# A gated-MLP stage in which four more pieces of the up projection move high and low input side by side, and every such piece runs its high weights before its low ones

## What is computed

```
def conv_gated_mlp(h, w_up, conv_w, w_down):
    u = h @ w_up                                   # 256 x 1024 times 1024 x 5632
    up = jnp.pad(u, ((0, 0), (pad, pad), (0, 0)))
    u = sum(up[:, t:t + S] * conv_w[t] for t in range(CONV_WIDTH))   # width 3
    gate, val = jnp.split(u, 2, axis=-1)
    return (jax.nn.gelu(gate, approximate=True) * val) @ w_down
...
for l in range(DEPTH):
    ...
    h = rms_norm(x, ffn_pre_norm[l])
    x = x + rms_norm(conv_gated_mlp(h, ...), ffn_post_norm[l])
```

## Time and profile before

| | us |
|---|---|
| median of 3 runs | 1020.44 |
| lowest, highest | 1019.81, 1020.45 |
| the profiled execution's own time | 1019.93 |
| its span, first to last instruction | 1018.1 |

### The profile page before, as it was taken

One profiled execution on the slowest core, in us unless ns is written; L12 is line 12 of the kernel. 1 busy time (PEld: TensorE's weight loads), 2 busy tenths in 40 slices (PEclk: granted clock), 3 DMA queues, 4 the chain that ended last, 5 costly groups with the idle time before them and its releaser, 6 DMA issues.

```text
span 1018.1 us, 14973 instructions
## 1 busy us (share of the span) xinstructions
PE 1004.8 (99%) x5744; PEld 880.4 (86%) x5744; DVE 711.1 (70%) x963; ACT 582.5 (57%) x863; POOL 128.8 (13%) x245
## 2 busy tenths in 40 slices
PE   8999999999999999999999999999999999999997
PEld 7889999888888988888888899998888889888886
DVE  6535566555586898989875355666545869898986
ACT  6657666555446655555575666565653456555552
POOL 3343124000001000000025231230000020000000
PEclk9999999999999999999999999999999999999999
DMA  7554345544445665555454544464335545655541
GB/s 243 198 174 157 124 129 180 168 166 158 136 141 166 205 230 176 196 195 178 150 178 158 173 127 125 140 222 154 131 130 186 183 147 188 214 200 191 182 165 42
DMA packets 108907, 170.74 MB, mean 168 GB/s; under 512 B 3249, under 2 KB 72676, under 8 KB 108836
## 3 DMA queue, kind: packets, MB, share of 16 engines
q1 hardware_dynamic: 107676, 166.88, 50.3%
q10 hardware_dynamic: 1080, 2.63, 0.7%
q0 software_dynamic: 80, 0.26, 0.1%
HBM read 168.72 MB, written 1.05 MB: 167 GB/s over the span
## 4 chain that ended last, share of the span: by engine, by line
PE 97%; DVE 1%; DMA 1%; ACT 0%; DVEq 0%; SPq 0%; issue 0%; POOL 0%; POOLq 0%
PE bank L1473 21%; PE bank L1475 20%; PE bank L1474 20%; PE high_banks L1483 10%; PE high_banks L1481 5%; PE high_banks L1913 2%; PE high_banks L1473 2%; PE high_banks L1474 2%; PE high_banks L1475 2%; PE high_banks L1480 1%; PE high_banks L1814 1%; PE high_banks L1835 1%; PE high_banks L1906 1%; PE high_banks L1823 1%; PE high_banks L1851 1%; PE high_banks L1858 1%
## 5 line engine op out<-in xcount | busy, mean ns | idle before, releaser
L1095 DVE TENSOR_TENSOR w_lo<-w_raw,w_hi 128x2048 fp32r<-128x2048 f32 (+3 forms) x174 | 365.1, 2100 | 162.8 <-ACT w_hi L721 162.7
L721 ACT ACTIVATE w_hi<-w_raw 128x2048 fp32r<-128x2048 f32 (+3 forms) x174 | 305.0, 1754 | 152.1 <-PE high_banks L1483 96.5
L1473 PE MATMUL bank<-w_hi,hT 128*128 128x512 f32 (+3 forms) x716 | 263.3, 368 | 2.0 <-DVE hT L1123 1.1
L1475 PE MATMUL bank<-w_hi,hT 128*128 128x512 f32 (+3 forms) x716 | 257.5, 360 | 0.0
L1474 PE MATMUL bank<-w_lo,hT 128*128 128x512 f32 (+3 forms) x716 | 257.1, 359 | 0.0
L1473 PEld LDWEIGHTS bank<-w_hi,hT 128*128 128x128 f32 x716 | 134.6, 188 | 18.4 <-issue 3.0
L1483 PE MATMUL high_banks<-hT,w_hi 128*128 128x512 f32 x420 | 149.7, 396 | 0.0
L1475 PEld LDWEIGHTS bank<-w_hi,hT 128*128 128x128 f32 x716 | 134.5, 188 | 14.0
L1474 PEld LDWEIGHTS bank<-w_lo,hT 128*128 128x128 f32 x716 | 134.7, 188 | 12.9
L1481 PE MATMUL high_banks<-hT,w_lo 128*128 128x256 f32 x480 | 124.0, 279 | 0.0
L1481 PEld LDWEIGHTS high_banks<-hT,w_lo 128*128 128x128 f32 x480 | 90.5, 188 | 5.2
(11 more groups left out here) (252 smaller groups left out, 1477.2 us busy)
## 6 DMA issues: line engine op xcount, KB each, us to landing
w_raw<-in_w_up_dram SPq DMA_DIRECT2D x44, 1024.0 KB, 5.0
w_raw<-in_w_in_dram SPq DMA_DIRECT2D x36, 1024.0 KB, 5.0
w_raw<-in_w_in_dram SPq DMA_DIRECT2D x36, 768.0 KB, 4.3
w_raw<-in_w_down_dram SPq DMA_DIRECT2D x22, 1024.0 KB, 4.8
w_raw<-in_w_out_dram SPq DMA_DIRECT2D x8, 1024.0 KB, 4.9
w_raw<-in_w_in_dram SPq DMA_DIRECT2D x8, 672.0 KB, 4.1
w_raw<-in_w_branch_mla_dram SPq DMA_DIRECT2D x4, 1024.0 KB, 4.9
w_raw<-in_w_branch_diff_dram SPq DMA_DIRECT2D x4, 1024.0 KB, 5.0
```

The source lines that it names most:

```text
L721: nc.scalar.activation(w_hi[:, n % RING, 0:nk * cols], raw[:, n % RING, 0:nk * cols], ACT.Copy).then_inc(hi_done, 1)
L1095: V.tensor_tensor(w_lo[:, n % RING, s], raw[:, n % RING, s], w_hi[:, n % RING, s].bitcast(F32), ALU.subtract).then_inc(lo_done, 1)
L1473: PE.matmul(dst, lhs[1], rhs_hi, start=start, stop=False)
L1475: return PE.matmul(dst, lhs[0], rhs_hi, start=False, stop=stop)
```

## The change

BESIDE goes from 6 to 2: up 2 to up 5 become wide, on TensorE and on VectorE. All wide pieces (up 2 to up 20) go through a new function, `up_beside`, which in each half issues the eight matmuls of the high weights and then the eight of the low ones. A wide piece waits for `hi_done` (ScalarE's part) at its start, and for `lo_done` (VectorE's part) only ahead of its first low matmul. The counts of `up_summed` follow BESIDE.

```diff
-BESIDE = 6
+BESIDE = 2
...
-            def passes_beside(dst, w_parts, k):
-
-                if k == 0:
-                    PE.matmul(dst, w_parts[0], hT[:, k, :, :], start=True, stop=False)
-                last = PE.matmul(dst[:, 0:SEQ], w_parts[1], hT_hi[:, k, :], start=False, stop=False)
-                if k:
-                    last = PE.matmul(dst, w_parts[0], hT[:, k, :, :], start=False, stop=k == KD - 1)
-                return last
+            def up_beside(l, n, c):
+
+                hi, lo = cut(w_hi, n), cut(w_lo, n)
+                for j in range(2):
+                    dst, cols = up_banks(c)[:, j, :], slice(j * P, (j + 1) * P)
+                    for k in range(KD):
+                        PE.matmul(dst, hi[:, k, cols], hT[:, k, :, :], start=k == 0, stop=False)
+                    if j == 0:
+                        pe.wait_ge(lo_done, l * NPIECE + (n + 1 + RING))
+                    for k in range(KD):
+                        last = PE.matmul(dst[:, 0:SEQ], lo[:, k, cols], hT_hi[:, k, :], start=False, stop=k == KD - 1)
+                last.then_inc(piece_used, 1)
...
-                pe.wait_ge(lo_done, l * NPIECE + (n + 1 + RING))
+                if kind == "up" and beside(c):
+                    pe.wait_ge(hi_done, l * NPIECE + (n + 1))
+                else:
+                    pe.wait_ge(lo_done, l * NPIECE + (n + 1 + RING))
```

More of the change, by code:

```diff
@@ L1623, in use_piece @@
                         pe.wait_ge(up_summed, l * (LAST_UP - BESIDE) + (c - 1 - BESIDE))
+                    if beside(c):
+                        up_beside(l, n, c)
+                        return
                     for k, j in [(k, j) for j in range(2) for k in range(8)]:
                         w_parts = (hi[:, k, j * P:(j + 1) * P], lo[:, k, j * P:(j + 1) * P])
[L1626 to L1629, removed]
+                        last = passes(up_half(c, j), w_parts, hT_hi[:, k, :], hT_lo[:, k, :], k == 0, k == 7)
                     last.then_inc(piece_used, 1)
```

## The result

| | before | after |
|---|---|---|
| median | 1020.26 | 1026.47 |
| lowest, highest (6 runs each) | 1019.63, 1020.55 | 1025.77, 1026.88 |
| the profiled execution | 1019.93 | 1026.45 |

The ratio is 1.0059, with a 95% interval of 1.0049 to 1.0069: the change costs 6.2 us. The forecast was 1025.2, the range 1022.4 to 1028.0.

What follows compares the result with a forecast made beforehand. TensorE was taken to bound the kernel, with VectorE nearly full from up 2 to up 5. Per layer +2.9 us at down 1 less 0.5 for the order, +2.4; both layers +4.8, giving 1025.2 us; range 1022.4 to 1028.0.

Steps and rivals of the forecast that it cites:

- The bound and the mechanism: TensorE, busy 99%, bounds the kernel; from up 2 nearly full VectorE gets more work and delays down 0 and down 1.
- TensorE's saving: Up 2 to up 5 wide: 0.68 us per layer in the old order; 1.44 with the new order on all wide pieces.
- Rivals 1 and 2: Down 0 and down 1 not held up, 1017.5 to 1019.0, chance 0.09; or smaller waits, a draw, 1018.5 to 1022.4, 0.09.
- The walk along VectorE's row: Up 2 to down 1: extra sums delay `g_lo`, so TensorE waits 2.5 us at down 0, 1.3 at down 1; 2.9 late.
- VectorE without a gap from up 2 to up 7: A sign expected in the new profile: VectorE's row runs on from up 2 to up 7, its earlier waits used up.
- The order of high and low: In wide up pieces, high then low makes a piece 5.55 us, not 5.59: 0.04 each, 0.5 us per layer after down 1.
- the second of the signs of being wrong: Wide up pieces stay at 5.59 us: the order brings nothing, and the time is 1 us above the forecast.
- Rival 4: More waits at up 6 or up 7, or the order gains nothing or costs: +5.8 to +7.5, 1026.2 to 1028; chance 0.16.
- The waits in both layers, and none later: TensorE waits about 2.5 us ahead of down 0 and 1.3 ahead of down 1, in both layers, and none later.
- rival 3: The wait at down 0 brings the 1.2 GHz clock: up to 5.5 us a time, 1030 or 1036; chance 0.04.

Runs made afterwards that it cites:

- experiments 5 and 6: The changed kernel, then the kernel before, each without VectorE's four convolution operations on up 2 to up 5: 1018.89 us and 1020.48 us.
- experiment 3: The kernel before, with an extra unused VectorE sum of about 1.3 us after the scaling of each of up 2 to up 5: 1026.55 us, ratio 1.0061.
- experiment 1: The changed kernel with BESIDE back at 6, so only the order of high and low in the 15 old wide pieces differs from before: 1020.11 us.
- experiment 9: The changed kernel with g_lo of pairs 0 and 1 and down 0's split moved earlier in VectorE's row: 1026.41 us, ratio 1.0063.
- experiment 8: The changed kernel with `gated` and `g_lo` of the first nine pairs moved from VectorE to GpSimd: 1022.89 us, ratio 1.0029.
- experiment 2: The kernel before with BESIDE 2: up 2 to up 5 wide, in the old order and with the old wait: 1026.50 us, ratio 1.0060.
- experiment 4: The kernel before with a smaller extra VectorE operation, some 0.6 us, on each of up 2 to up 5: 1020.59 us, ratio 1.0002.
- experiment 7: The changed kernel with BESIDE 4: up 2 and up 3 narrow, in other PSUM banks: 1021.50 us, ratio 1.0010.
- experiment 10: The changed kernel with BESIDE 5: only up 5 wide in addition, up 2 to up 4 narrow: 1020.12 us, ratio 0.9996.

## Why the prediction was right

**The bound and the mechanism.** Right. TensorE's saving is real (experiments 5 and 6) and worth nothing, since VectorE's row decides when down 0 and down 1 start (experiment 3). Rivals 1 and 2 are out.

**The walk along VectorE's row.** With the 0.48 us taken off, `g_lo` of pair 0 starts at 361.9 (forecast 362.10), down 0 at 362.7 (362.9), `g_lo` of pair 1 at 379.93 (379.9), down 1 at 380.8 (380.7). The sum and the product last 1.92 us on up 4 (358.24 to 360.16), and so on all four pieces; for up 2 and up 4 I had 2.01, from a row in which VectorE had just waited. That is 0.2 us less by `g_lo`. The 0.45 us gap with the name "issue" ahead of up 5's convolution was used up, as taken; one like it that I had not foreseen, 0.43 us, opened in up 4's (364.44), in the first layer only, so that the two errors nearly cancel at down 1. That this start came out to 0.1 us is luck in part. By the starts, TensorE was ready for down 0 four times 5.58 us after up 2, at 360.87, and waited 2.27 us (the profile's 2.09 counts from a modelled end); forecast 2.5. Ahead of down 1 it was 1.23 for 1.3.

**VectorE without a gap from up 2 to up 7.** Right but for that 0.43 us; it waits for TensorE first at up 8 (0.66 us, at 392.52).

**The order of high and low.** This step failed, and it is the second of the signs of being wrong that the prediction names (1 us above the forecast; it was 1.3). I gave it 0.04 us a piece, from the duration of a matmul in a down piece, and so 0.5 us back in each layer after down 1. The pieces last 5.58 us, 0.01 less than before, and experiment 1 gives nothing. The layer is late by 3.0 us at down 2 as at down 1, and by 497.76 - 494.34 - 0.48 = 2.9 us where down 8 starts, right behind the last up piece: next to nothing comes back. With this term at 0.1 instead of 0.5 the sum is 2 x 2.8 = 5.6 us. The mis-sized price is that of a 512 in an up piece: eight take 340.39 - 338.55 = 1.84 us, 0.230 each, not the 0.227 of a down piece, which moves other operands. With the eight 256s in 0.95 us that is 0.349 us a pair, against the 0.35 of before; 0.003 us on 16 matmuls was all that I had built the gain on.

**The size.** Forecast +4.8, measured +6.2. Of the 1.4 between them 0.8 are the order (5.6 for 4.8). Up to the start of down 8, counted from the start of the stretch, the first layer is 2.98 us late and the second 3.11, 6.1 in all. Of the 0.5 between that and 5.6 the clock, below, may account for all, by an estimate of 0.5 us; the walk's own errors, such as the gap of 0.43 us in the first layer alone, are of the same size, so I leave the split open. The 0.1 from 6.1 to 6.2 is less than what the medians of the kernel before differ by (1020.20 to 1020.52). Rival 4 in its mildest form, the order worth nothing (+5.8 to +7.5), is what happened to the sum: the measured 1026.47 lies among its times, 1026.2 to 1028, to which I gave 0.16, and in my range only because that takes it in.

**The waits in both layers, and none later.** Right for down 0, wrong for down 1 of the second layer, and that is what **rival 3** had foreseen, which I gave 0.04, though not at its price. After the wait of 2.10 us in the second layer the granted clock fell. Windows of the changed kernel: stretch, length, busy us per engine (PE, PEld, DVE, ACT, POOL), clock, DMA share, GB/s:

```profile
866.00:867.00 1.00, 0.45 (x2) 0.43 (x3) 0.91 (x3) 0.39 (x1) 0.00 (x0) 0.97 0.16 20
867.00:868.00 1.00, 1.00 (x4) 0.78 (x3) 0.93 (x4) 0.00 (x0) 0.00 (x0) 0.50 0.62 156
...
869.00:870.00 1.00, 1.00 (x4) 0.81 (x3) 0.91 (x2) 0.00 (x0) 0.00 (x0) 0.50 1.03 426
870.00:871.00 1.00, 1.00 (x5) 0.78 (x5) 1.00 (x3) 0.67 (x2) 0.00 (x0) 0.82 0.17 57
```

And the timeline of PE there, with down 0's first matmul, two from the slow stretch, the start of up 6, and down 1:

```profile
866.55 0.47 PE L1473 MATMUL bank<-w_hi,g_lo 128*128 128x512 f32 x1 [2.10 <-DVE w_lo L1095]
...
867.62 0.63 PE L1473 MATMUL bank<-w_hi,g_lo 128*128 128x512 f32 x1
868.05 0.63 PE L1474 MATMUL bank<-w_lo,g_hi 128*128 128x512 f32 x1
...
873.70 0.39 PE L1483 MATMUL high_banks<-hT,w_hi 128*128 128x512 f32 x1
...
884.85 0.40 PE L1473 MATMUL bank<-w_hi,g_lo 128*128 128x512 f32 x1
```

At 0.50, the 1.2 GHz level, matmuls stand 0.43 us apart instead of 0.227, and down 0 lasts 873.70 - 866.55 = 7.15 us, 1.6 more than the 5.56 of the first layer. I had priced this at up to 5.5 us. It cost little: TensorE would have waited at down 1 until VectorE was done with `g_lo` (at 884.36) in any case, and starts it at 884.85 instead. VectorE's row there, from the convolution on up 4 over the sum on up 6 to `g_lo` of pair 1:

```profile
867.49 0.88 DVE L1430 SCALAR_TENSOR_TENSOR conv_out<-up_scaled,par_all,conv_out 128x255 f32<-128x255 f32 x2
...
879.46 1.23 DVE L1155 TENSOR_REDUCE up_scaled<-high_banks 128x512 f32<-128x1024 f32 x1
...
883.68 0.68 DVE L1170 TENSOR_TENSOR g_lo<-conv_out,g_hi 128x512 fp32r<-128x512 f32 x1
```

From down 0 to down 1 it is 18.30 us here and 18.10 in the first layer. These 18.10 hold the gap ahead of L1430, though (1.31 us from L1424 to it, against 0.95 here), so the difference of 0.2 does not tell the price. Without the slow stretch VectorE would have come to up 6's sum 0.1 us earlier and gone through it without the 0.1 that it takes after a wait, and down 1 would have started some 0.15 behind `g_lo`, as in the first layer: at 884.3 instead of 884.85. My estimate from these rows is therefore 0.5 us. The clock ate for the most part a wait that was already lost.

My argument against rival 3, that the clock never left the full level in any slice, was weak. A slice is 25.6 us long, and the line of the changed kernel shows a 9 in all 40 slices too, with 3.4 us at 0.50 in one of them.

## What to carry to other kernels

Before work is moved from a full engine to another, walk along the other's row, operation by operation, to the first result that the full engine needs; the cover there (here 2.1 us, less what the full engine comes earlier), and not the mean load over the stage, says how much it may take. Where both of two adjoining waits end with the same engine, savings in between count for nothing, and neither does a loss there that is smaller than the second wait. A gain that rests on a few thousandths of a microsecond between matmuls of different operands (here 0.04 us a piece for an order of instructions) is entered at nothing until rows of the same operands show it.

## What the runs showed of the hardware

- A wait of TensorE of 2.10 us (the changed kernel, second layer) and one of 2.32 us (experiment 9, first layer) were each followed by some 3.4 us at a granted clock of 0.50. Waits of 2.09 us (the changed kernel, first layer), 1.95 and 1.91 us (experiments 9 and 8) were not. At the start of the program, where the wait ahead of the first matmul on `x_rows` (L1749 before, L1756 after) differs from one profile to the next, waits of 1.93 us (experiment 2) and 2.30 (experiment 4) were followed by such a fall, at 9.66 us, and waits of 2.64 (experiment 7) and 2.41 (experiment 10) were not. Length alone does not decide it; what else does was not tried. Windows of experiment 9, in the same columns as above:

```profile
371.00:372.00 1.00, 1.00 (x9) 1.00 (x10) 0.93 (x3) 1.00 (x2) 0.00 (x0) 1.00 0.07 10
372.00:373.00 1.00, 1.00 (x5) 0.77 (x4) 1.00 (x3) 1.00 (x1) 0.00 (x0) 0.56 0.93 206
```

- The fall does not come in the wait but behind it, when TensorE is working again: some 0.4 us later in the one case (work from 866.55, 0.97 for the window to 867.00), 1.3 us in the other (work from 370.83, full clock to 372.00, 0.56 for the window behind). A matmul that runs slowly may answer to a wait well ahead of it.
- GpSimd and VectorE took turns on two-input operations: 0.93 us more on a VectorE pair of 0.88, 1.10 on two splits of 4.48, and 3.21 instead of 1.3 for the GpSimd operation in between (experiment 8). Beside a sum out of PSUM neither was slowed.
